# Router on scaled, unnormalised activations in a two-layer hybrid backbone: logits transposed, the norm factor as a token column, the shift added after the gather

## The reference, cut to what matters

```python
x = x + g1 * merge_branches(proj, attn, lp)
h2 = rmsnorm(x, norm2_g) * (1 + sc2) + sh2
logits = h2 @ router                    # 8 experts
top_v, top_i = lax.top_k(logits, 2)
wts = softmax(top_v)
x = x + g2 * sum_e comb[:, e] * ((silu(h2 @ w1[e]) * (h2 @ w3[e])) @ w2[e])
```

## Time and profile before

| | |
|---|---|
| median of 3 runs | 2185.57 us (2185.32 to 2186.03) |
| profiled execution | 2185.18 us, span 2183.4 us |
| TensorE busy | 2094.0 us, 96% |
| VectorE busy | 1768.7 us, 81% |
| ScalarE busy | 1176.1 us, 54% |
| GpSimd busy | 42.6 us, 2% |
| chain that ended last | PE 83%, DVE 10%, issue 2%, ACT 2%, DMA 1% |

### The profile page before, as it was taken

One profiled execution on the slowest core, in us unless ns is written; L12 is line 12 of the kernel. 1 busy time (PEld: TensorE's weight loads), 2 busy tenths in 40 slices (PEclk: granted clock), 3 DMA queues, 4 the chain that ended last, 5 costly groups with the idle time before them and its releaser, 6 DMA issues.

```text
span 2183.4 us, 28769 instructions
## 1 busy us (share of the span) xinstructions
PE 2094.0 (96%) x10186; PEld 1732.2 (79%) x10186; DVE 1768.7 (81%) x2235; ACT 1176.1 (54%) x1388; POOL 42.6 (2%) x84
## 2 busy tenths in 40 slices
PE   8999999997999998889998999999999999999997
PEld 6765888866888887759997888888888888888886
DVE  7786877978677676877866989899898989999895
ACT  3316233324333332534555777777777777777773
POOL 0000000000000000000000000000000000000000
PEclk9999999998999999899997999999999999999999
DMA  8500233553444443403463999989898999989893
GB/s 323 193 34 1 97 111 135 183 193 116 173 154 154 172 154 115 163 25 124 165 242 151 366 359 353 371 330 383 336 374 342 374 356 354 380 322 385 332 375 117
DMA packets 77289, 512.44 MB, mean 235 GB/s; under 512 B 8738, under 2 KB 9890, under 8 KB 22820
## 3 DMA queue, kind: packets, MB, share of 16 engines
q1 hardware_dynamic: 65700, 469.59, 56.8%
q0 software_dynamic: 11520, 41.95, 5.4%
HBM read 510.46 MB, written 1.05 MB: 234 GB/s over the span
## 4 chain that ended last, share of the span: by engine, by line
PE 83%; DVE 10%; issue 2%; ACT 2%; DMA 1%; SPq 0%; DVEq 0%; ACTq 0%; POOL 0%; POOLq 0%
PE bank L856 9%; PE bank L854 9%; PE bank L855 9%; PE bank L875 5%; PE bank L876 5%; PE bank L877 5%; PE bank L599 4%; PE bank L601 4%; PE bank L600 4%; DVE tile_low L1405 2%; PE bank L764 2%; PE bank L765 2%; PE bank L766 2%; PE bank L740 2%; PE bank L750 2%
## 5 line engine op out<-in xcount | busy, mean ns | idle before, releaser
L983 ACT ACTIVATE down_high<-W 128x1024 fp32r<-128x1024 f32 x224 | 236.9, 1063 | 124.7 <-PE bank L877 124.5
L1354 DVE TENSOR_TENSOR up_b_low<-W,up_b_high 128x2048 fp32r<-128x2048 f32 x112 | 256.5, 2290 | 53.3 <-ACT up_b_high L976 53.3
L1361 DVE TENSOR_TENSOR down_low<-W,down_high 128x1024 fp32r<-128x1024 f32 x224 | 270.5, 1222 | 23.4 <-ACT down_high L983 9.1
L1348 DVE TENSOR_TENSOR up_a_low<-W,up_a_high 128x2048 fp32r<-128x2048 f32 x112 | 255.8, 2284 | 1.9 <-ACT up_a_high L970 1.9
L599 PE MATMUL bank<-h_high,tile_high 128*128 128x512 f32 (+1 forms) x704 | 238.2, 338 | 0.8 <-DVE tile_low L1405 0.8
L600 PE MATMUL bank<-h_low,tile_high 128*128 128x512 f32 (+1 forms) x704 | 236.5, 336 | 0.0
L601 PE MATMUL bank<-h_high,tile_low 128*128 128x512 f32 (+1 forms) x704 | 236.4, 336 | 0.0
L970 ACT ACTIVATE up_a_high<-W 128x2048 fp32r<-128x2048 f32 x112 | 212.9, 1901 | 2.1 <-PE bank L856 2.1
L976 ACT ACTIVATE up_b_high<-W 128x2048 fp32r<-128x2048 f32 x112 | 213.2, 1904 | 0.0
L875 PE MATMUL bank<-down_high,mact_high 128*128 128x512 f32 x448 | 183.5, 410 | 2.6 <-DVE down_low L1361 2.6
L854 PE MATMUL bank<-up_a_high,gathered_high 128*128 128x512 f32 x448 | 174.5, 389 | 1.4 <-DVE gathered_low L1743 1.4
(11 more groups left out here) (260 smaller groups left out, 4326.3 us busy)
## 6 DMA issues: line engine op xcount, KB each, us to landing
W<-in_moe_up SPq DMA_DIRECT2D x224, 1024.0 KB, 6.8
W<-in_moe_down SPq DMA_DIRECT2D x112, 1024.0 KB, 6.5
W<-in_w_mod_later POOLq DMA_DIRECT2D x80, 512.0 KB, 3.8
W<-in_ffn SPq DMA_DIRECT2D x33, 1024.0 KB, 4.8
W<-in_attn_blocks SPq DMA_DIRECT2D x24, 1280.0 KB, 6.0
W<-in_attn_blocks SPq DMA_DIRECT2D x22, 1024.0 KB, 5.7
W<-in_attn_blocks SPq DMA_DIRECT2D x8, 1536.0 KB, 6.6
shift_tiles<-in_w_mod_first SPq DMA_DIRECT2D x8, 512.0 KB, 14.2
```

Source lines behind the costliest of these rows:

```text
L1348: tt(al[u][:], raw_a[u].rearrange("p (k n) -> p k n", k=KD // 2), ah[u][:].bitcast(F32), ALU.subtract) \
L1354: tt(bl[u][:], raw_b[u].rearrange("p (k n) -> p k n", k=KD // 2), bh[u][:].bitcast(F32), ALU.subtract) \
L1361: tt(cl[:, h, :], raw_c[u][:, h * D:(h + 1) * D], ch[:, h, :].bitcast(F32), ALU.subtract) \
```

## The change

The norm's factor of a token is left out of the activations, and brought in later.

- `router_logits` takes the place of `sum_squares` and of the logits in layer 2. ACT writes `xs`, the residual times the channel's factor (`x_scaled`), behind each square. The router is the weight and `xs` moves (8x256 per tile, so the logits come out with experts on partitions); DVE keeps them in `logits_row`, two transposes bring them back to tokens on partitions. The sum of squares comes out as one column for each token tile, and its root and reciprocal (`R[:, ROOT]`, `R[:, RSTD]`) have two columns.
- Logits are the turned ones times the token's factor, plus the product of router and shift, which DVE forms ahead (`router_shift`) and TensorE sums over the channels (`logit_shift`).
- `htok` is the transposed `xs`, scaled by the token's factor as ACT copies it. The shift is added to the gathered tokens, for each tile of channels as its own column: so `gathered_high` and `gathered_low` are four 128x128 instructions for each bank in place of one 128x512. This holds for all nine gathers.
- `up` waits for each half of the gathered tokens where it needs it, in place of both ahead.
- `choose` handles both token tiles at once, with five steps in place of eight.
- `up_b_low(0, 0)` and `up_a_low(1, 1)` moved on DVE, and `up_a_high(1, 1)` on ACT; the overflow test (`over`) moved behind the selection.

```diff
+    order += [f"out{KD - 1}"]
+    if layer == 0:
+        return order + ["norm2"]
+    return order + ["logit_shift", "logits", "norm2", "tokens0", "turned_logits", "tokens1", "tokens2", "tokens3", "rank", "over"]
...
+        xs = at("x_scaled", [KD, LAT], shared + 4 * D)
+        router_shift = at("router_shift", [KD, E], late)
+        logits_row = at("logits_row", [LAT], rstd_at, parts=E)
...
+            def router_logits(layer):
+                ni = NORMS.index((layer, "norm2"))
+                pe.wait_ge(S("router_in"), 16)
+                pe.wait_ge(S("router_shifted"), 1)
+                b = opened(layer, "logit_shift")
+                done(layer, "logit_shift", mm(b[:, 0:E], C("ones"), R[:, SHIFTED, 0, :], start=True, stop=True))
+                logits = opened(layer, "logits")
+                def logit(k):
+                    pe.wait_ge(S("x_scaled"), k + 1)
+                    return mm(logits[0:E, 0:LAT], router[:, k, :], xs[:, k, :], start=k == 0, stop=k == KD - 1)
+                for k in range(KD - 2):
+                    logit(k)
+                sums = opened(layer, "norm2")
+                pe.wait_ge(S("square_used"), (ni + 1) * (KD - 1))
+                pe.wait_ge(S("square_ready"), (ni + 1) * KD)
+                for t in range(2):
+                    mm(sums[:, t:t + 1], root[:, t * P:(t + 1) * P], C("ones")[:, 0:1], start=True, stop=False)
+                    last = mm(sums[:, t:t + 1], nsq[:, 1, t * P:(t + 1) * P], C("ones")[:, 0:1], start=False, stop=True)
+                done(layer, "norm2", last)
+                logit(KD - 2)
+                done(layer, "logits", logit(KD - 1))
+                for r in range(4):
+                    if r == 1:
+                        pe.wait_ge(S("logits_kept"), 1)
+                        b = opened(layer, "turned_logits")
+                        for t in range(2):
+                            last = pe.transpose(b[:, t * E:(t + 1) * E], logits_row[0:E, t * P:(t + 1) * P], C("ident")[0:E, 0:E])
+                        done(layer, "turned_logits", last)
+                    hf, t = divmod(r, 2)
+                    b = opened(layer, f"tokens{r}")
+                    for kk in range(4):
+                        last = pe.transpose(b[:, kk * P:(kk + 1) * P], xs[:, 4 * hf + kk, t * P:(t + 1) * P], C("ident"))
+                    done(layer, f"tokens{r}", last)
+                pe.wait_ge(S("mask_ready"), 1)
+                m = R[:, MASK]
+                b = opened(layer, "rank")
+                mm(b[:, 0:E], C("below"), m[:, 0, :], start=True, stop=True)
+                mm(b[:, E:2 * E], C("ones"), m[:, 0, :], start=True, stop=False)
+                done(layer, "rank", mm(b[:, E:2 * E], C("below"), m[:, 1, :], start=False, stop=True))
+                b = opened(layer, "over")
+                mm(b[:, 0:E], C("ones"), m[:, 0, :], start=True, stop=False)
+                done(layer, "over", mm(b[:, 0:E], C("ones"), m[:, 1, :], start=False, stop=True))
...
-            pe.wait_ge(S("router_in"), 16)
-            for k in range(KD):
-                pe.wait_ge(S("h_ready"), H_BEFORE[1, "norm2"] + k + 1)
-                for t in range(2):
-                    logit = mm(banks[6 * t][:, 0:E], hT[:, k, t * P:(t + 1) * P], router[:, k, :], start=k == 0, stop=k == KD - 1)
-                if k == KD - 1:
-                    logit.then_inc(S("logits_full"), 1)
-                hf, kk = divmod(k, 4)
-                for t in range(2):
-                    last = pe.transpose(banks[1 + 2 * hf + t][:, kk * P:(kk + 1) * P], hT[:, k, t * P:(t + 1) * P], C("ident"))
-                    if kk == 3:
-                        last.then_inc(S("htok_full"), 1)
...
+                def up(g, u, gathered=None):
                     b = banks[u]
                     pe.wait_ge(S("up_a_low"), g + 1)
                     for k in range(KD):
+                        if gathered is not None and k % (KD // 2) == 0:
+                            pe.wait_ge(S("gathered_low"), gathered + (k // (KD // 2) + 1))
...
+                    if layer and name == "norm2":
+                        fn(xs[:, k, :], xT[:, k, 0:n], ACT.Copy, scale=scale[:, 1, k, 0:1]).then_inc(S("x_scaled"), 1)
...
+                if layer and name == "norm2":
+                    fn(R[:, ROOT, 0, 0:2], b[:, 0:2], ACT.Sqrt, bias=C("eps"), scale=1.0 / D).then_inc(free(layer, name), 1)
+                    up_b_high(0, 0, 0)
+                    return
...
+            act.wait_ge(S("token_rstd"), 1)
+            for r in range(4):
+                hf, t = divmod(r, 2)
+                b = filled(act, 1, f"tokens{r}")
+                fn(htok[:, t, hf * 512:(hf + 1) * 512], b[:, :], ACT.Copy, scale=R[:, RSTD, 0, t:t + 1]) \
+                    .then_inc(free(1, f"tokens{r}"), 1)
             up_a_high(1, 1, 0)
-            for r in range(4):
-                act.wait_ge(S("htok_full"), r + 1)
-                hf, t = divmod(r, 2)
-                fn(htok[:, t, hf * 512:(hf + 1) * 512], banks[1 + r][:, :], ACT.Copy).then_inc(S("htok_ready"), 1)
...
-                    fn(hgh[:, 4 * hf:4 * hf + 4, :], banks[6 + hf][:, :].rearrange("p (k s) -> p k s", k=4), ACT.Copy) \
-                        .then_inc(S("gathered_high"), 1)
+                    for kk in range(4):
+                        k = 4 * hf + kk
+                        last = fn(hgh[:, k, :], banks[6 + hf][:, kk * P:(kk + 1) * P], ACT.Identity, bias=modT[:, 1, 3 * KD + k, 0:1])
+                    last.then_inc(S("gathered_high"), 1)
...
+                    shift = modT[:, 1, 3 * KD:4 * KD, 0].unsqueeze(2).broadcast_to([P, KD, E])
+                    step(tt(router_shift[:, :, :], router[:, :, :], shift, ALU.mult))
+                    dve.tensor_reduce(R[:, SHIFTED, 0], router_shift[:, :, :].rearrange("p k e -> p e k"), AX, ALU.add) \
+                        .then_inc(S("router_shifted"), 1)
...
-            up_b_low(0, 0)
-            up_a_low(1, 1)
-            dve.wait_ge(S("logits_full"), 1)
+            b = filled(dve, 1, "logit_shift")
+            dve.tensor_copy(R[:, SHIFT, 0], b[:, 0:E]).then_inc(free(1, "logit_shift"), 1)
+            b = filled(dve, 1, "logits")
+            dve.tensor_copy(logits_row[0:E, :], b[0:E, 0:LAT]).then_inc(S("logits_kept"), 1)
+            dve.sem_inc(free(1, "logits"), 1)
+            read(dve, 1, "norm2")
+            dve.reciprocal(R[:, RSTD, 0, 0:2], R[:, ROOT, 0, 0:2]).then_inc(S("token_rstd"), 1)
+            dve.wait_ge(S("token_rstd"), 1)
+            read(dve, 1, "logit_shift")
+            b = filled(dve, 1, "turned_logits")
             for t in range(2):
-                step(dve.tensor_copy(R[:, LOGITS, t], banks[6 * t][:, 0:E]))
-            iota8 = C("iota8")
+                last = stt(out=R[:, LOGITS, t], in0=b[:, t * E:(t + 1) * E], scalar=R[:, RSTD, 0, t:t + 1], in1=R[:, SHIFT, 0],
+                           op0=ALU.mult, op1=ALU.add)
+            last.then_inc(free(1, "turned_logits"), 1)
+            read(dve, 1, "turned_logits")
+            iota8 = C("iota8").unsqueeze(1).broadcast_to([P, 2, E])
             top = R[:, TOP, 0]
             def choose(src, one, at):
-                for t in range(2):
-                    step(dve.tensor_reduce(top[:, at + t:at + t + 1], R[:, src, t], AX, ALU.max))
-                    step(stt(out=R[:, EQUAL, t], in0=R[:, src, t], scalar=top[:, at + t:at + t + 1], in1=iota8,
-                             op0=ALU.is_equal, op1=ALU.mult))
-                    step(dve.tensor_reduce(top[:, 6 + t:7 + t], R[:, EQUAL, t], AX, ALU.max))
-                    step(ts(R[:, one, t], R[:, EQUAL, t], top[:, 6 + t:7 + t], None, ALU.is_equal))
+                step(dve.tensor_reduce(top[:, at:at + 2], R[:, src], AX, ALU.max))
+                step(tt(R[:, EQUAL], R[:, src], top[:, at:at + 2].unsqueeze(2).broadcast_to([P, 2, E]), ALU.is_equal))
+                step(tt(R[:, EQUAL], R[:, EQUAL], iota8, ALU.mult))
+                step(dve.tensor_reduce(top[:, 6:8], R[:, EQUAL], AX, ALU.max))
+                step(tt(R[:, one], R[:, EQUAL], top[:, 6:8].unsqueeze(2).broadcast_to([P, 2, E]), ALU.is_equal))
...
             dve.wait_ge(S("mask_ready"), 1)
             tt(R[:, GAP, 0, 0:2], top[:, 2:4], top[:, 0:2], ALU.subtract).then_inc(S("gap_ready"), 1)
-            dve.wait_ge(S("rank_full"), 1)
             step(ts(R[:, EQUAL], R[:, MASK], -1.0, 1000.0, ALU.add, ALU.mult))
-            step(tt(R[:, RANK], banks[5][:, 0:2 * E].rearrange("p (t e) -> p t e", t=2), R[:, MASK], ALU.mult))
+            up_b_low(0, 0)
+            ranks = filled(dve, 1, "rank")
+            tt(R[:, RANK], ranks[:, 0:2 * E].rearrange("p (t e) -> p t e", t=2), R[:, MASK], ALU.mult).then_inc(free(1, "rank"), 1)
+            read(dve, 1, "rank")
...
+            def overflow():
+                b = filled(dve, 1, "over")
+                dve.tensor_reduce(over_f[:, :], b[:, 0:E], AX, ALU.max).then_inc(free(1, "over"), 1)
+                read(dve, 1, "over")
```

(20 more changed lines are left out.)

42 lines of the change are left out of this document (14 added, 28 removed).

## The result

The changed kernel takes 2171.99 us (median of 4 runs, 2170.78 to 2172.3), the kernel before 2185.45 beside it (4 runs, 2184.91 to 2186.03). The ratio of after to before is 0.9935, with a 95% interval of 0.9923 to 0.9947: 14.2 us less by the ratio (11.6 to 16.8 by its interval), 13.5 by the medians. I had forecast 2174.3, and 2171.5 to 2178.5. The ratio on the time that I had started from (2185.57) comes to 2171.4, which is 0.1 beyond the range's fast edge. The profiled execution took 2172.3, span 2170.5.

A forecast was written before the change was run, and what follows sets the result against it. TensorE, busy 96% of the span, bounds the kernel, so only its idle or low-clock places count. Relay saving 11.9 less 0.6 in the tail gives 11.3, so 2174.3 us from 2185.57; range 2171.5 to 2178.5.

The forecast's parts named there:

- The relay: From last output projection to first expert matmul, engines working one at a time: first expert matmul at 1163.0, saving 11.9 us.
- Logits full: Router product on TensorE after the last projection: dense passes at high clock, 0.21 us per 256-wide pass, done at 1148.7.
- the rival of a low clock already in the logits: Narrow sums let TensorE's clock fall while the logits are formed: time 2176.4, chance 0.12.
- Mask: Choice of two experts on DVE: eleven steps for seventeen, 2.45 us against 4.07, mask at 1152.55.
- up_b_low bare on the path: DVE does this split (2.28 us) after the mask and ahead of the ranks, adding to the path, to 1155.25.
- Gather: TensorE's first gather starts at 1156.45; at low clock its first half takes 3.82 us, full at 1160.3.
- The rival of a high clock: TensorE keeps the high clock through the first gather: time 2173.4, chance 0.12.
- Split in pieces: Gathered tokens split in four 128x128 pieces a half: ACT 1.27 us for four, DVE 1.3.
- Boundaries: Seven changes of expert: the split gathers are ready before TensorE wants them, cost zero.
- The rival on the other side: Split gathers stall every expert boundary, TensorE waiting above 1.14 us a pair; at 1.9, about 2195. Chance 0.02.
- The weight stream: Rival: weight transfers limit the expert stage, so the earlier start does not move the end: 2185, chance 0.04.
- Tail: Behind the last gather: its split stands before the last products, so down_low starts 0.6 us later, cost 0.6.

The follow-up runs named there:

- e1: Changed kernel with the choice of two experts made one token tile after the other (17 small steps in place of 11): 2173.21 us, ratio 0.9945.
- e4: Changed kernel with up_b_low(0,0) moved behind the selection and up_a_low(1,1) behind the split of the gathered tokens: 2172.71 us, ratio 0.9948.
- e11: e4 with the 32 one-column passes of the token weights split into two groups of 16: 2168.8 us, ratio 0.9929.
- e2: Changed kernel, but each expert's up matmuls wait at their start for both halves of the gathered tokens: 2176.81 us, ratio 0.9961.
- e10: Kernel before with the 32 one-column passes split into two groups of 16, one ahead of each half of the turns of Pm: 2182.37 us, ratio 0.9988.
- e3: Changed kernel with the shift left out of the gathered tokens and one 128x512 instruction a bank in place of four pieces: 2172.46 us, ratio 0.9946.
- e5: Changed kernel with logits formed untransposed on x_scaled, eight columns in two token tiles, no copy, no turn: 2173.16 us, ratio 0.995.
- e8: Changed kernel with the edits of e4 and e5 together: 2170.65 us, ratio 0.9942.
- e9: Changed kernel with the 32 one-column passes split into two groups of 16, one ahead of each half of the turns of Pm: 2170.91 us, ratio 0.9936.

## Why the prediction came out as it did

**The relay: right, nearly term by term.** Predicted 18.93 from the issue after the last projection to the first expert matmul (1144.07 to 1163.0), measured 19.07 (1145.30 to 1164.37). Luck has a share in so small a difference: the gather began 0.4 later than by the sum (12.8 for 12.4), and the split of the first half, with its hand-overs, took 0.2 less. And the saving of 11.9 hangs on the trace that it is taken from: 11.8 and 12.6 in the two pairs, since the kernel before had 30.99 and 31.82. From the first of these marks:
- Logits full: 4.6 predicted, 4.9 measured. Dense passes at 1.00, as I had taken them, at 0.224 each (2.69 for 12) where I had 0.21; the rival of a low clock already in the logits did not come.
- Mask: ready 8.5 after it by the prediction, 8.7 measured. e1 confirms the choice, 1.62 for the steps that became fewer.
- up_b_low bare on the path: 2.29 as priced. e4 and e11 take it off and the relay loses 1.5, not 2.3, because the rank matmuls come out from behind it.
- Gather: 3.77 for the first half at 0.50, predicted 3.82. The rival of a high clock did not come: the clock dropped at 1155.5.
- Split in pieces: ACT 1.14 for four where I had 1.27, DVE 1.13 where I had 1.3. Interpolating between near rows was 11 and 15% high. An estimate from the figures of the Trainium skill (ScalarE: Activation LUTs, "What ACT_TABLE_LOAD costs") gives 1.27 for ACT as well; the trace has 1.14 to 1.15 at all places and decides.

**Boundaries: right.** Zero predicted. The four pieces and four behind them are ready 2.2 us early (1284.02 for 1286.27), and e2 shows none of seven boundaries to wait even for both halves. The 862.26 that hold them are the same in all kernels, with and without the split. The rival on the other side is far off: it needed 1.14 a pair, and a pair takes 0.57. The weight stream did not give the gain back.

**Tail: wrong in size.** 0.6 predicted; down_low starts 6.66 after the start of the last gather (2148.65 - 2141.99), before it was 6.53, so 0.13 later. The pieces were shorter, and I had overlooked a gap: before, DVE stood idle for 0.78 ahead of down_low, waiting for ACT's down_high. The product came 1.0 later behind its gather (2147.99 - 2141.99 = 6.00, before 2159.24 - 2154.23 = 5.01) and mostly filled that gap.

**The step that failed: the stage taken as before but for the tail.** With zero at the boundaries and 0.6 in the tail, the sum left all else in the expert stage as it was. I priced only what the diff touches. The token weights, 32 one-column passes, lie in expert 0 in both kernels and no line of them is in the diff. In the kernel before the clock falls behind them in both traces, from 1195.6 and 1196.4, in the changed kernel in neither. The stage was 2.3 shorter in place of 0.6 longer in the first pair of traces, 1.2 shorter in the second. In both, 1.7 of it is expert 0, with the passes in it; the rest, 0.6 shorter and 0.5 longer, is the end, where executions of one kernel differ as much. e10 shows the cause for the kernel before: divide the passes and 1.8 comes back in expert 0, 2.0 in the whole stage. The rows were there to be read: I took the 3.63 for 32 passes as a price, and the 1.76 for eight turns stood in the trace right behind it. I took the duration and did not ask about the clock. The range had the same hole: its terms are pieces and the clock in the relay, and none is for the clock in the stage.

**What stays open.** Why the changed kernel escapes this fall with the same undivided passes, and e3, e4 and e5 do not. The passes come 16.9 us after the first expert matmul in both kernels (1191.87 - 1174.94, 1181.29 - 1164.37), so their place in the stage is not it. Sorted by relay, undivided passes lost the clock in four kernels of 17.38 to 18.79 (e8, e5, e3, e4), kept it in four traces of 19.19 to 21.41 (the changed kernel twice, e1, e2), and lost it in two of 31. The time since the clock's last rise sorts them as well: kept at 18.5 to 18.9, lost at 17.4 to 17.9 and at 19.3 to 20.2. Only e2, with a stretch at 0.50 of its own in between, kept it at 15.2. Read so, the change did not take the fall away by what it does, but moved the passes against the rise, and an edit as small as e3's (0.4 us of relay) moves them back. Both sortings were found after the runs, and that the history of the clock before the experts decides is a guess that no run tested. And with two traces of either kernel it isn't shown that the change as such removes the fall; what is shown is that a fall there costs 1.6 to 3.3 us in expert 0, and that dividing the passes removes it in four kernels of four. The 1 to 4 us ahead of the relay differ between executions of one kernel and belong to no part of the change.

## What to carry to other kernels

Walk a chain in which engines take turns instruction by instruction from the rows: over 19 us here the sum was off by 0.14 us, no single mark in it by more than 0.4. Then, for everything a diff leaves alone but shifts in time, read the granted clock too: here it fell in or behind runs of passes of one and of eight columns, though TensorE was busy all the time, and what followed ran at half rate. Dealing such passes out between wider matmuls cost nothing and kept the stage within 0.4 us in four kernels. And compare two kernels stretch by stretch: here the stretch that holds all seven boundaries of experts was equal to 0.01 us, so all the difference of the stages had to lie in the first expert and at the end.

## What I had not expected of the hardware

- The clock fell while TensorE was busy without a gap: 4.00 of 4.00 us busy at 0.81, then at 0.50, in and behind the one-column passes (e4, above). So with e5's logits of eight columns, dense from 1141.16, in this window of it, while the same product 256 columns wide kept 1.00:

```profile
1145.00:1149.00 4.00, 4.00 (x21) 4.00 (x21) 2.62 (x15) 3.45 (x5) 0.00 (x0) 0.51 0.05 20
```

- 32 passes of one column take 3.63 in both kernels and 4.40 in e4, where the clock fell among them; divided, two times 1.84 (e9).
- One kernel's executions differ with nothing changed, the kernel before by 5 us from its fastest to its slowest; changes of 1.5 us in a relay are read from the trace, not from the times.
